# Two-map attention with half of its constant products, ScalarE's copy ahead of the exponentials, a second score pair, and far-level copies on ScalarE

## The reference, cut to what matters

```
s = jnp.einsum('bhcqd,bhckd->bhcqk', qi, kt)      # c = 0, 1: two maps of one head
p = jax.nn.softmax(jnp.where(mask, s, NEG_BIG), axis=-1)
a = p[:, :, 0] - lam * p[:, :, 1]
return jnp.einsum('bhqk,bhkv->bhqv', a, v)
```

## Time and profile before

| | |
|---|---|
| median of 3 runs | 3455.8 us (3455.28 to 3464.26) |
| the profiled execution | 3460.29 us, of which the span is 3458.5 us |
| mean granted clock of TensorE | 0.993 |
| TensorE busy | 3409.3 us, 99% of the span |
| VectorE, ScalarE, GpSimd busy | 1392.7, 1012.4, 1509.7 us |

### The profile page before, as it was taken

One profiled execution on the slowest core, in us unless ns is written; L12 is line 12 of the kernel. 1 busy time (PEld: TensorE's weight loads), 2 busy tenths in 40 slices (PEclk: granted clock), 3 DMA queues, 4 the chain that ended last, 5 costly groups with the idle time before them and its releaser, 6 DMA issues.

```text
span 3458.5 us, 41815 instructions
## 1 busy us (share of the span) xinstructions
PE 3409.3 (99%) x16720; PEld 2748.0 (79%) x16720; DVE 1392.7 (40%) x2596; ACT 1012.4 (29%) x1275; POOL 1509.7 (44%) x522
## 2 busy tenths in 40 slices
PE   8999999899999999999999999999999999999999
PEld 7878877688888888886888887867888878778887
DVE  6565248745253524146212026854101158541010
ACT  3222322732123212224222233443212234432121
POOL 3545552045455545540354564502646545025453
PEclk9999999999999999999999999999999999999999
DMA  7444322034343543311223222201222222012222
GB/s 287 181 154 180 103 86 74 1 122 179 140 186 115 191 144 142 100 48 66 73 86 104 89 99 73 75 24 49 98 97 97 97 73 74 25 49 98 97 96 75
DMA packets 58748, 358.65 MB, mean 104 GB/s; under 512 B 10208, under 2 KB 10592, under 8 KB 21856
## 3 DMA queue, kind: packets, MB, share of 16 engines
q1 hardware_dynamic: 58592, 356.50, 28.8%
HBM read 354.38 MB, written 2.10 MB: 103 GB/s over the span
## 4 chain that ended last, share of the span: by engine, by line
PE 95%; DVE 3%; issue 1%; DMA 1%; ACT 1%; SPq 0%; POOL 0%; DVEq 0%; ACTq 0%
PE LP L576 85%; PE XB L576 9%; DMA big<-w_ada 1%; PE LP L954 0%; PE XB L799 0%; DVE XB L2070 0%; PE XB L835 0%; ACT E L1355 0%; DVE big L2463 0%; DVE E L2473 0%; DVE S L2426 0%; DVE big L2252 0%; DVE big L2250 0%; DVE big L2249 0%; DVE w_lo L2129 0%
## 5 line engine op out<-in xcount | busy, mean ns | idle before, releaser
L1857 POOL TENSOR_TENSOR w_lo<-ring,w_hi 128x2048 fp32r<-128x2048 f32 (+3 forms) x275 | 1134.1, 4124 | 700.8 <-ACT w_hi L1355 700.8
L576 PE MATMUL LP<-u_hi,w_hi 128*128 128x512 f32 x2448 | 958.8, 392 | 2.6 <-ACT u_hi L1355 2.4
L576 PE MATMUL LP<-u_hi,w_lo 128*128 128x512 f32 x2448 | 953.6, 390 | 0.0
L576 PE MATMUL LP<-u_lo,w_hi 128*128 128x512 f32 x2448 | 935.2, 391 | 0.0
L576 PE MATMUL LP<-big_r,w_hi 128*128 128x512 f32 x2520 | 780.4, 390 | 5.0 <-DVE h L2317 2.5
L1355 ACT ACTIVATE w_hi<-ring 128x2048 fp32r<-128x2048 f32 (+3 forms) x275 | 474.4, 1725 | 749.4 <-PE LP L576 746.5
L576 PE MATMUL LP<-big_r,w_lo 128*128 128x512 f32 x1508 | 587.5, 390 | 0.0
L576 PEld LDWEIGHTS LP<-big_r,w_hi 128*128 128x128 f32 x2520 | 472.8, 188 | 106.0 <-DVE h L2317 4.2
L576 PEld LDWEIGHTS LP<-u_hi,w_hi 128*128 128x128 f32 x2448 | 460.1, 188 | 111.7 <-issue 16.1
L576 PEld LDWEIGHTS LP<-u_lo,w_hi 128*128 128x128 f32 x2448 | 462.5, 189 | 95.6 <-issue 0.5
L576 PEld LDWEIGHTS LP<-u_hi,w_lo 128*128 128x128 f32 x2448 | 460.1, 188 | 95.9
(11 more groups left out here) (360 smaller groups left out, 3475.2 us busy)
## 6 DMA issues: line engine op xcount, KB each, us to landing
ada_in<-w_ada SPq DMA_DIRECT2D x66, 1024.0 KB, 4.9
ring<-w_in SPq DMA_DIRECT2D x20, 1024.0 KB, 4.8
ring<-w_gu00a SPq DMA_DIRECT2D x11, 1024.0 KB, 7.0
ring<-w_gu00b SPq DMA_DIRECT2D x11, 1024.0 KB, 6.5
ring<-w_gu01a SPq DMA_DIRECT2D x11, 1024.0 KB, 6.7
ring<-w_gu01b SPq DMA_DIRECT2D x11, 1024.0 KB, 6.7
ring<-w_gu10a SPq DMA_DIRECT2D x11, 1024.0 KB, 6.7
ring<-w_gu10b SPq DMA_DIRECT2D x11, 1024.0 KB, 5.0
```

Of the source, the lines that this page charges most:

```text
L576: return pe.matmul(o, lhsT=lhsT, rhs=rhs, start=start, stop=stop)
L1857: gp.tensor_tensor(w_lo[:, slab % RING, 0:width], ring[:, slab % RING, 0:width], w_high(q, width).bitcast(F32), ALU.subtract).then_inc(s(" ...
```

## The change

- `fill_heads` in the two-map attention issues 15 products of constants in each layer where it issued 29: at steps 0, 2, 6, 9, 13 and 16 fewer, at steps 8, 11 and 18 none.
- ScalarE's copy of unit `n - 2` stands ahead of the exponentials of unit `n`.
- The masked scores of odd units go into `big[:, HF:HF + 2]` instead of `S`, and VectorE waits for the exponentials of two units before, not of the last. Ahead of the attention VectorE waits for its own last `x_ready`, since that place is read until then.
- The three far copies (four instructions) of each layer go from VectorE to ScalarE, behind its exponentials of steps 1, 3 and 5.

```diff
+        def diff_masked(n):
+
+            return big[:, HF:HF + 2, :] if n % 2 else S
...
-                    fill_heads(n, {0: 5, 2: 5, 6: 2, 8: 2, 9: 3, 11: 2, 13: 3, 16: 5, 18: 2}.get(n, 0))
+                    fill_heads(n, {0: 4, 2: 4, 6: 1, 9: 2, 13: 1, 16: 3}.get(n, 0))
...
                 for n in range(n_units + 2):
+                    if n >= 2:
+                        i, W = n - 2, ((n - 2) % NB + 1) * P
+                        act.wait_ge(s("transposed"), p0 + i + 1)
+                        if i >= 2:
+                            act.wait_ge(s("pv_done"), p0 + i - 1)
+                        f(ET[:, i % 2, 0:W], XB[3][:, 0:W], ACT.Copy).then_inc(s("pt_done"), 1)
...
-                            f(E[:, k % 4, 0:W], S[:, m, 0:W], ACT.Exp, scale=-1.0, bias=stat[:, k % 4, 0:1],
+                            f(E[:, k % 4, 0:W], diff_masked(n)[:, m, 0:W], ACT.Exp, scale=-1.0, bias=stat[:, k % 4, 0:1],
...
+                def far_taken(n):
+
+                    if n == 1:
+                        pl.got("far_mm")
+                        for cp in range(2):
+                            o = OD[cp].rearrange("p j (i t) -> p j i t", t=P)[:, :, 0:6:5, :]
+                            i = LP[1][:, :, 256 * cp:256 * cp + 256].rearrange("p j (i t) -> p j i t", t=P)
+                            ins = f(o, i, ACT.Copy)
+                        ins.then_inc(s("far_taken"), 1)
+                    if n in (3, 5):
+                        pl.got("far_mm")
+                        f(OD[(n - 3) // 2][:, :, P:640], LP[1][:, :, :], ACT.Copy).then_inc(s("far_taken"), 1)
...
-                            if n:
-                                dve.wait_ge(s("diff_exp"), u0 + k - 1)
+                            if n >= 2:
+                                dve.wait_ge(s("diff_exp"), u0 + k - 3)
...
+                dve.wait_ge(s("x_ready"), 9 * (l + 1))
                 diff_attention(l, 2, st[:, 50 + l:51 + l], beside_maps)
```

More of the change, by code:

```diff
@@ L1786, in memory_exp @@
                           bias=tokw[:, 4 * b + hh:4 * b + hh + 1]).then_inc(s("me_done"), 1)
+                def far_taken(n):
[9 more added lines that the diff above has]
+                        f(OD[(n - 3) // 2][:, :, P:640], LP[1][:, :, :], ACT.Copy).then_inc(s("far_taken"), 1)
                 def beside_maps(n):
+                    far_taken(n)
                     if n == 9:
@@ L2386, in diff_attention @@
                             dve.wait_ge(s("diff_scores"), u0 + k + 1)
-                            if n:
-                                dve.wait_ge(s("diff_exp"), u0 + k - 1)
+                            if n >= 2:
+                                dve.wait_ge(s("diff_exp"), u0 + k - 3)
                             dve.tensor_tensor_reduce(
-                                out=S[:, m, 0:W], in0=XB[k % 3][:, 0:W], in1=cc("causal", T - W, W), scale=1.0,
+                                out=diff_masked(n)[:, m, 0:W], in0=XB[k % 3][:, 0:W], in1=cc("causal", T - W, W), scale=1.0,
                                 scalar=-LOWEST, op0=ALU.add, op1=ALU.min, accum_out=stat[:, k % 4, 0:1])\
@@ L2856, in values_taken, with far_mixed @@
                         conv(3)
[L2858 to L2869, removed]
+                def far_mixed(n):
                     if n == 8:
@@ L2896, in beside_maps @@
                 def beside_maps(n):
-                    far_taken(n)
+                    far_mixed(n)
                     if n in (13, 14):
```

## The result

| | before | after |
|---|---|---|
| median | 3459.43 us (3455.28 to 3464.37, 20 runs) | 3462.74 us (3459.78 to 3471.25, 20 runs) |
| ratio to before | | 1.0013, 95% interval 1.0007 to 1.0019 |
| profiled execution, its span | 3460.29, 3458.5 | 3460.63, 3458.8 |
| TensorE busy | 3409.3 us | 3399.8 us |

The changed kernel is slower, by 0.07 to 0.19%: a loss of 2.4 to 6.6 us, small but real. The forecast was 3454.6 us, a gain of 1.2 us. But twenty runs of each kernel tell more than that, and the sign was wrong.

A forecast was written before the change was run, and what follows sets the result against it. TensorE, busy 99% of the span, bounds the kernel. Seven attention stretches win 2.2 us per layer, 0.6 with one half-clock stretch kept, 1.2 in all: 3454.6 us, range 3447 to 3464.

The forecast's parts named there:

- The cost of a constant: TensorE's queue in the attention: each product 0.43 us, each group 0.21 more; removals free 6.65 us per layer.
- The walk of the waits: Attention in seven stretches, asking what TensorE waits for without the constants: 59.5 us against 61.7 per layer without clock falls.
- stretch three: Recurrence's output of step 6 to gate rows of step 9: 1.50 us of constants become wait, 12.4 us against 12.53.
- stretch four: Gate rows of step 9 to those of step 11: ScalarE's new order makes it 7.9 us against 7.28, 0.65 slower.
- The double scores at nothing: VectorE may start the next masked scores early; costed at no gain, bounds 0 and 1 us won per layer.
- the far copy between its bounds: Far copy ahead of step 4's far products, moved to ScalarE: priced between 1.00 us (ScalarE) and 1.22 us (VectorE).
- I take one fall of the present size per layer in place of the present one: Attention: one half-clock stretch per layer, some 1.6 us lost, as now; leaves 0.6 us won per layer.
- the sum: Attention's seven stretches added: 2.2 us won per layer without half clock, 0.6 with one half-clock stretch as now.
- stretch five: Gate rows of step 11 to step 13: constants 0.86 us less, wait 1.1, so +0.2 on 5.98, 6.2 us.
- the prediction's own signs of being wrong: Attention of 55 us or less per layer, PEclk under 0.9 over the whole attention, or time moving in untouched stages.
- The third rival: Steps 8 to 13: clock stays low behind waits before 4-row products; +4.7 us per layer, 3465 us; chance 0.22.
- The rule on transposes: Step 9's gate rows to attention's end at half clock without constants among transposes; 3498 us, chance 0.02.

The follow-up runs named there:

- e2: The changed kernel with the old table of 29 constants per layer, so the new queues alone; 3458.64 us, 1.0007 of before.
- e6: The changed kernel with the old table of 29 constants and ScalarE's copy behind the exponentials again; 3460.30 us, 1.0004 of before.
- e9: The kernel before, queues untouched, with 23 constants per layer placed where TensorE waits or has thin work behind; 3454.38 us, 0.9987 of before.
- e8: The changed kernel with ScalarE's copy behind the exponentials and 23 constants placed at waits or ahead of thin work; 3446.12 us, 0.9968 of before.
- e3: The changed kernel with four constants more at step 18, just ahead of the sums of squares; 3461.01 us, 1.0012 of before.
- e7: The kernel before with four constants more at step 4, inside TensorE's wait of 2.51 us; 3459.92 us, 1.0002 of before.
- e1: The kernel before with the new table of 15 constants alone, queues untouched; 3462.28 us, 1.0017 of before.

## Why the prediction was wrong, step by step

- **The cost of a constant held** (0.43 each, 0.21 per group). Busy time of TensorE fell by 9.5, not the 13 of the prediction, and for the most part elsewhere. Products at half clock are busy for longer: in the attentions and sums of both layers busy time fell by only 1.3 us (134.7 to 133.3), which is 13.3 less by the constants and 11.9 more by seven falls more at 1.7. The rest of the 9.5 fits the falls outside that the profile of after hasn't.
- **The walk of the waits held.** Far products 2.1 forecast, 2.04 measured; step 6, 0.5 and 0.43; step 11, 1.7 and 1.67; step 16, 0.9 and 0.99; step 18, 1.0 and 0.90; and the 1.50 of stretch three is a wait of 1.46 for the probabilities. ScalarE's order costs what stretch four said: 7.9 against 8.01, and e2 has the queues at 0.5 us per layer with the clock unmoved. The wait of 1.1 at step 13 was hidden by half clock in the first layer.
- **The double scores at nothing** and the far copy between its bounds fit the stretches they touch in the change (13.00 and 5.85). The two weren't taken apart; e6 has both with the old table (1.0004, nothing that can be told), e9 against e8 with the placed one (7 us).
- **The step that failed** is "I take one fall of the present size per layer in place of the present one". The term that it sized, the clock's, was carried as unchanged. The changed kernel has two falls in the first layer's attention and three in the second's, and three instead of one in the sums of each: over the runs 10.8 us more lost in all, 5.4 per layer, where the sum had 0. The net is only 2.5 per layer, since a part of the lost time is hidden: in the first layer the fall in stretch three added 1.2 us to the forecast, and that in stretch five 0.4, since it ran out in the wait of 1.1 for the gate rows. Two falls, 3.4 us lost, cost 1.6 there, and 59.5 + 1.6 is 61.1 where 61.31 was measured. What is hidden in this way would be what the rest wins beyond the 0.6 of the sum, 2.3 per layer over the runs; that fits the 1.8 of the first layer, but wasn't tested.
- **The sums were not walked**, because the change doesn't touch them. They hold the largest single piece, 3.25 us per layer in the profiles; time moving in such a stage was one of the prediction's own signs of being wrong. The two constants at step 18 and those at step 16 had stood just ahead of them; e3 brings it back by constants alone.
- **The third rival had the mechanism**: half clock behind new waits next to 4-row products, from step 8 to 13. I gave it 0.22 and priced it at 4.7 per layer, twice what the runs show net. The evidence for it stood in the prediction, the 14 us at 593 without any idle time, and I set it against waits of 1.40 in other attentions that had kept the clock. Those waits lie among products of 64 rows and more.
- **The rule on transposes**: transposes alone didn't bring down the clock over the attention (0.94 and 0.92 after, not half). The Trainium skill, "TensorE: Matmul & The Clock Gate", section "Part 4: PE-mode transpose", says that transposes don't count as busy time in the way other products do. If that holds, the constants among them weigh more than their time. The series 29, 15, 0 with 0.97, 0.94, 0.80 in the first attention would fit that as well as it fits idle time alone; no run here takes the two apart.

What stays open is which moment decides where a fall lands: e6's first layer and e7's new fall weren't foreseen, and the same waits at step 4 had a fall behind them or none. Open is also which of the constants taken out cost the attention its clock, since only those ahead of the sums were put back by themselves (e3).

## What to carry to other kernels

Products of constants inside a wait cost no time (e7) and can keep the clock up; the same products on the path cost their full time. So first read where TensorE waits, put them there, and read again when any other queue changes, since a table fits one order of the queues. Then walk also what comes behind: thin stretches that the change doesn't touch can pay for it. A change of a few products is judged by the mean granted clock of many runs and not by one pair of profiles, where falls elsewhere come and go by more than the effect.

## What the runs showed of the hardware

- The length of a wait didn't settle the clock behind it. In after's first layer falls came behind waits of 1.46 and 1.67 us (0.66 over 2288 to 2293, 0.57 over 2302 to 2306); waits of 1.40 elsewhere kept 1.00, and so did the wait of 2.51 in e1, which had a fall behind it before.
- The clock stayed at half for about 10 us (0.54 over 2322 to 2333) with TensorE busy throughout, in products of width 1 and 2; 24 records of width 1 took 5.00 us for 2.82.
- Falls lost nearly the same everywhere, 1.7 us or a multiple of it: 1.7, 3.4 or 5.1 in the attentions and sums of after.
- Part of a fall can be hidden: in after's first layer two falls, 3.4 us lost, made the attention 1.6 us longer than the walk without a fall.
- Taking one fall away need not take its cost away: in e7 one of the same size came 27 us later in the same layer.
